# Both Fourier transforms of a transformer trunk over even and odd inputs at 128 frequencies, with the halves combined behind the second one

## What is computed

```
def fourier_mixer(h, w_in, w_out):
    B, S, D = h.shape                                  # 1, 256, 1024
    u = (h @ w_in).reshape(B, S, 4, 256)
    f = jnp.fft.fft2(u.astype(jnp.float32), axes=(1, 3), norm="ortho").real
    return f.astype(h.dtype).reshape(B, S, D) @ w_out
```

## Time and profile before

| | |
|---|---|
| median of 3 runs | 1410.08 us (1409.67 to 1410.91) |
| profiled execution, its own time | 1411.13 us |
| its span, first to last instruction | 1409.3 us |
| mean granted TensorE clock | 0.994 of full |
| PE busy | 1388.9 us (99%), 6511 matmul records |
| DVE busy, ACT busy | 1127.1 us (80%), 926.1 us (66%) |
| HBM | 418.47 MB read, 298 GB/s over the span |

### The profile page before, as it was taken

The page is one execution under the profiler, slowest core; times in us unless marked ns, Lnnn a source line. Parts: engine busy times, 40 slices in busy tenths (PEclk is TensorE's granted clock), DMA queues, the critical chain, the costliest instruction groups (busy, mean ns, idle before and its releaser), DMA issues.

```text
span 1409.3 us, 17766 instructions
## 1 busy us (share of the span) xinstructions
PE 1388.9 (99%) x6511; PEld 1151.1 (82%) x6511; DVE 1127.1 (80%) x811; ACT 926.1 (66%) x760; POOL 20.0 (1%) x29
## 2 busy tenths in 40 slices
PE   9999999999979999999999999999999999999997
PEld 8888888787868888888888888888888888888885
DVE  6455666655668889888988988898898889889887
ACT  6353444444656777777777777777777777777774
POOL 0000000000030000000000000000000000000000
PEclk9999999999989999999999999999999999999999
DMA  9367775563148999999999999999999999999992
GB/s 356 132 179 221 220 202 179 172 198 109 32 140 313 361 375 340 359 377 354 356 362 375 334 362 374 357 357 376 366 329 377 363 354 350 368 375 333 372 375 90
DMA packets 191689, 420.10 MB, mean 298 GB/s; under 512 B 19168, under 2 KB 21344, under 8 KB 191648
## 3 DMA queue, kind: packets, MB, share of 16 engines
q1 hardware_dynamic: 178432, 415.00, 81.9%
q10 hardware_dynamic: 12784, 3.26, 1.7%
q0 software_dynamic: 432, 1.28, 0.3%
HBM read 418.47 MB, written 1.05 MB: 298 GB/s over the span
## 4 chain that ended last, share of the span: by engine, by line
PE 97%; DVE 1%; ACT 1%; DMA 1%; issue 0%; POOL 0%; POOLq 0%; SPq 0%; DVEq 0%; ACTq 0%
PE bank_G L1061 10%; PE bank_G L1063 10%; PE bank_G L1062 10%; PE bank_U L1061 10%; PE bank_U L1063 10%; PE bank_U L1062 10%; PE bank_Y L1061 8%; PE bank_Y L1063 8%; PE bank_Y L1062 8%; PE bank_T L1418 2%; PE bank_G L1310 1%; PE bank_T L1061 1%; PE bank_T L1063 1%; PE bank_T L1062 1%; PE bank_T L1321 1%; PE bank_G L1379 1%
## 5 line engine op out<-in xcount | busy, mean ns | idle before, releaser
L674 DVE TENSOR_TENSOR w_lo<-raw,w_hi 128x2048 fp32r<-128x2048 f32 x390 | 888.0, 2290 | 197.7 <-ACT w_hi L400 197.6
L400 ACT ACTIVATE w_hi<-raw 128x2048 fp32r<-128x2048 f32 x390 | 748.2, 1919 | 284.3 <-PE bank_U L1063 102.1
L1061 PE MATMUL bank_Y<-w_hi,hidT_hi 128*128 128x512 f32 x492 | 192.3, 391 | 0.0
L1063 PE MATMUL bank_Y<-w_hi,hidT_lo 128*128 128x512 f32 x492 | 191.6, 389 | 0.0
L1062 PE MATMUL bank_Y<-w_lo,hidT_hi 128*128 128x512 f32 x492 | 191.4, 389 | 0.0
L1061 PE MATMUL bank_U<-w_hi,xg_hi 128*128 128x512 f32 x448 | 179.1, 400 | 0.0
L1061 PE MATMUL bank_G<-w_hi,xg_hi 128*128 128x512 f32 x448 | 175.7, 392 | 0.7 <-DVE w_lo L674 0.5
L1063 PE MATMUL bank_U<-w_hi,xg_lo 128*128 128x512 f32 x448 | 175.0, 391 | 0.0
L1063 PE MATMUL bank_G<-w_hi,xg_lo 128*128 128x512 f32 x448 | 174.8, 390 | 0.0
L1062 PE MATMUL bank_G<-w_lo,xg_hi 128*128 128x512 f32 x448 | 174.7, 390 | 0.0
L1062 PE MATMUL bank_U<-w_lo,xg_hi 128*128 128x512 f32 x448 | 174.6, 390 | 0.0
(11 more groups left out here) (264 smaller groups left out, 1471.1 us busy)
## 6 DMA issues: line engine op xcount, KB each, us to landing
raw<-in_expert_w_gate SPq DMA_DIRECT2D x112, 1024.0 KB, 7.0
raw<-in_expert_w_up SPq DMA_DIRECT2D x112, 1024.0 KB, 7.0
raw<-in_expert_w_down SPq DMA_DIRECT2D x112, 1024.0 KB, 6.8
raw<-in_nat_w_qkv SPq DMA_DIRECT2D x12, 1024.0 KB, 5.1
raw<-in_ffn_w_gate SPq DMA_DIRECT2D x11, 1024.0 KB, 7.9
raw<-in_ffn_w_up SPq DMA_DIRECT2D x11, 1024.0 KB, 6.0
raw<-in_ffn_w_down SPq DMA_DIRECT2D x11, 1024.0 KB, 5.2
raw<-in_fourier_w_in SPq DMA_DIRECT2D x4, 1024.0 KB, 11.5
```

The lines of the kernel that those rows point to most:

```text
L400: nc.scalar.activation(w_hi[w][:], raw[s][:], ACT.Copy).then_inc(hi_made, 1)
L674: nc.vector.tensor_tensor(w_lo[w][:], raw[s][:], w_hi[w][:].bitcast(f32), ALU.subtract).then_inc(lo_made, 1)
L1061: nc.tensor.matmul(out_, xh, wh, start=start, stop=False)
L1063: return nc.tensor.matmul(out_, xl, wh, start=False, stop=stop)
```

## The change

A 256-point sum over inputs splits into a sum over even inputs and one over odd inputs; the second half of the output frequencies is the first sum minus the second. Both transforms are now made so, at 128 frequencies:

- x is loaded a first time into `x_turns` with token 2p+b in partition p, so that block b is the tokens of one parity, and a second time into `h`, behind the table, for the addition at the end. The table has 3 x 128 columns, its rows sorted even first.
- `u_hi` and `u_lo` are written with the even channels of a group before the odd ones: the reads of the banks step by two elements (`by_parity`).
- `token_dft` gives 128 cosines and 128 sines for each token parity b, side by side in the bank and not accumulated: 6 matmuls of 256 columns.
- `channel_dft(g)` gives, for the even channels (r = 0) and the odd ones (r = 1), 128 frequencies of the group: 12 matmuls of 256 columns for a whole group, into one bank Y[g % 2]. The moving operand is taken in two runs of 128 columns.
- ScalarE copies the odd half to SBUF (`odd`). VectorE's `fold` adds and subtracts it (`by_channel`, two operations of 256 elements), then adds and subtracts the token parities (`by_token`, two more). ScalarE and VectorE make `act_hi` and `act_lo` of a group at once, 512 elements, one turn of the loop later.
- The projection's first piece waits for two groups, its second piece for all four.

Cut to its core:

```diff
+    fo |= layout([("x_turns", [P, NB, D], f32), ("dft_raw", [P, NB, 3 * P], f32)],
+                 arena_start + sum(width_of(shape) for _, shape, _ in fourier_l[:4]))
+    def by_parity(bk):
+        return bk[:].rearrange("p (j r) -> p r j", r=2)
+    def u_part(t, c, b):
+        return t[:, b, BANK * c:BANK * (c + 1)].rearrange("p (r j) -> p r j", r=2)
...
         for c in range(2):
-            sp.dma_start(h[:, :, cs], x[0, :, cs].rearrange("(b p) d -> p b d", p=P)).then_inc(s_x[c], 16)
+            sp.dma_start(fo["x_turns"][:, :, cs], x[0, :, cs].rearrange("(p b) d -> p b d", b=NB)).then_inc(s_x[c], 16)
...
             if j == 3:
                 sp.dma_start(fo["dft_raw"][:], dft_c.rearrange("(b p) n -> p b n", p=P)).then_inc(s_dft, 16)
+                sp.dma_start(h[:], x[0].rearrange("(b p) d -> p b d", p=P)).then_inc(s_h, 16)
...
-                nc.scalar.activation(fo["u_hi"][:, b, BANK * c:BANK * (c + 1)], (G, U)[c][b][:], ACT.Copy,
+                nc.scalar.activation(u_part(fo["u_hi"], c, b), by_parity((G, U)[c][b]), ACT.Copy,
...
-        for g in range(KD // 2 + 1):
-            for m in (2 * g, 2 * g + 1) if g < KD // 2 else ():
+        for g in range(GROUPS + 2):
+            for m in (2 * g, 2 * g + 1) if g < GROUPS else ():
                 act.wait_ge(pt_psum, m + 1)
                 if m >= PT:
-                    act.wait_ge(ft_psum, m // 2 * 2 - PT + 2)
+                    act.wait_ge(ft_psum, (m - PT) // 2 + 1)
                 nc.scalar.activation(fo["pt_hi"][:, m % PT], T[m % 2][:], ACT.Copy).then_inc(pt_hi_done, 1)
-            for m in (2 * g - 2, 2 * g - 1) if g else ():
-                act.wait_ge(ft_psum, m + 1)
-                nc.scalar.activation(act_hi[:, m], Y[m % 2][:, :S], ACT.Copy).then_inc(ft_hi_done, 1)
+            if g >= 2:
+                act.wait_ge(ft_tokens, 2 * (g - 1))
+                nc.scalar.activation(act_hi[:, 2 * g - 4:2 * g - 2],
+                                     fo["by_token"][:, g % 2].rearrange("p k b t -> p k (b t)"), ACT.Copy).then_inc(ft_hi_done, 1)
+            if 1 <= g < GROUPS + 1:
+                act.wait_ge(ft_psum, g)
+                if g >= 3:
+                    act.wait_ge(ft_channels, 2 * (g - 2))
+                nc.scalar.activation(fo["odd"][:, (g - 1) % 2], Y[(g - 1) % 2][:, S:], ACT.Copy).then_inc(ft_odd, 1)
...
+            if pieces is at["w_out"]:
+                dve.wait_ge(s_h, 16)
...
+        def fold(g):
+            even, odd = Y[g % 2][:, :S], fo["odd"][:, g % 2]
+            channels, tokens = fo["by_channel"][:, g % 2], fo["by_token"][:, g % 2]
+            dve.wait_ge(ft_odd, g + 1)
+            for n, op in enumerate((ALU.add, ALU.subtract)):
+                nc.vector.tensor_tensor(channels[:, n].rearrange("p b t -> p (b t)"), even, odd, op).then_inc(ft_channels, 1)
+            dve.wait_ge(ft_channels, 2 * (g + 1))
+            for n, op in enumerate((ALU.add, ALU.subtract)):
+                nc.vector.tensor_tensor(tokens[:, :, n], channels[:, :, 0], channels[:, :, 1], op).then_inc(ft_tokens, 1)
...
             for b in range(NB):
-                last = three(T[m % 2][:], fo["u_hi"][:, b, P * m:P * (m + 1)], fo["u_lo"][:, b, P * m:P * (m + 1)],
-                             fo["dft_hi"][:, b, 0:2 * S], fo["dft_lo"][:, b, 0:2 * S], b == 0, b == NB - 1)
+                last = three(T[m % 2][:, S * b:S * (b + 1)], fo["u_hi"][:, b, o:o + P], fo["u_lo"][:, b, o:o + P],
+                             fo["dft_hi"][:, b, 0:S], fo["dft_lo"][:, b, 0:S], True, True)
...
+        def channel_dft(g):
+            pe.wait_ge(pt_lo_done, 2 * g + 2)
+            if g >= 2:
+                pe.wait_ge(ft_channels, 2 * (g - 1))
+            for r in range(2):
+                for part in range(2):
+                    o = (0, S)[part]
+                    moving = [fo[name][:, (2 * g + r) % PT].rearrange("p (b f t) -> p b f t", b=NB, f=2)[:, :, part]
+                              for name in ("pt_hi", "pt_lo")]
+                    last = three(Y[g % 2][:, S * r:S * (r + 1)].rearrange("p (b t) -> p b t", b=NB),
+                                 fo["dft_hi"][:, r, o:o + P], fo["dft_lo"][:, r, o:o + P], *moving, part == 0, part == 1)
             last.then_inc(ft_psum, 1)
...
-        pe.wait_ge(ft_lo_done, KD)
-        project(at["w_out"][0], G, BANK, fo_psum)
+        def folded(n, b):
+            if b == 0:
+                pe.wait_ge(ft_lo_done, GROUPS // 2 * (n + 1))
+        project(at["w_out"][0], G, BANK, fo_psum, folded)
```

More of the change, by code:

```diff
@@ L177, in trunk @@
     bias_l = [("bias", [P, HEADS * SHIFTS, GRID], f32)]
-    fourier_l = [("dft_hi", [P, NB, 3 * S], f32r), ("dft_lo", [P, NB, 3 * S], f32r),
+    fourier_l = [("dft_hi", [P, NB, 3 * P], f32r), ("dft_lo", [P, NB, 3 * P], f32r),
                  ("u_hi", [P, NB, D], f32r), ("u_lo", [P, NB, D], f32r),
-                 ("pt_lo", [P, PT, 2 * S], f32r), ("pt_hi", [P, PT, 2 * S], f32r)]
+                 ("pt_lo", [P, PT, 2 * S], f32r), ("pt_hi", [P, PT, 2 * S], f32r),
+                 ("odd", [P, 2, S], f32), ("by_channel", [P, 2, 2, NB, P], f32), ("by_token", [P, 2, 2, NB, P], f32)]
     attn_l = bias_l + [("qT", [P, KD, S], f32), ("kT", [P, KD, S], f32),
@@ L231, in trunk @@
     s_x = [sem(f"s_x{c}") for c in range(2)]
+    s_h = sem("s_h")
     h_half, sq_done, rstd_chain, rstd_done, hn_done = (sem(n) for n in (
@@ L743, in _ @@
                 dve.wait_ge(u_hi_done, NB * c + b + 1)
-                cs = slice(BANK * c, BANK * (c + 1))
-                rest_scaled(fo["u_lo"][:, b, cs], (G, U)[c][b][:], rstd[:, 0, b:b + 1], fo["u_hi"][:, b, cs]).then_inc(u_lo_done, 1)
+                rest_scaled(u_part(fo["u_lo"], c, b), by_parity((G, U)[c][b]), rstd[:, 0, b:b + 1], u_part(fo["u_hi"], c, b)).then_inc(u_lo_done, 1)
             if c == 0:
@@ L748, in _ @@
                 rest(fo["dft_lo"][:], fo["dft_raw"][:], fo["dft_hi"][:]).then_inc(dft_lo_done, 1)
-        for g in range(KD // 2 + 1):
-            for m in (2 * g, 2 * g + 1) if g < KD // 2 else ():
+        def fold(g):
[7 more added lines that the diff above has]
+                nc.vector.tensor_tensor(tokens[:, :, n], channels[:, :, 0], channels[:, :, 1], op).then_inc(ft_tokens, 1)
+        for g in range(GROUPS + 2):
+            for m in (2 * g, 2 * g + 1) if g < GROUPS else ():
                 dve.wait_ge(pt_hi_done, m + 1)
                 rest(fo["pt_lo"][:, m % PT], T[m % 2][:], fo["pt_hi"][:, m % PT]).then_inc(pt_lo_done, 1)
-            for m in (2 * g - 2, 2 * g - 1) if g else ():
-                dve.wait_ge(ft_hi_done, m + 1)
-                rest(act_lo[:, m], Y[m % 2][:, :S], act_hi[:, m]).then_inc(ft_lo_done, 1)
+            if g >= 2:
+                dve.wait_ge(ft_hi_done, g - 1)
+                rest(act_lo[:, 2 * g - 4:2 * g - 2], fo["by_token"][:, g % 2].rearrange("p k b t -> p k (b t)"),
+                     act_hi[:, 2 * g - 4:2 * g - 2]).then_inc(ft_lo_done, 1)
+            if 1 <= g < GROUPS + 1:
+                fold(g - 1)
         n = at["w_out"][0][-1]
@@ L1098, in transpose_stream @@
                         kk = 2 * q + k
-                        last = nc.tensor.transpose(STREAM[i][q][:, o:o + P], h[:, b, P * kk:P * (kk + 1)], ident[:])
+                        of = h if i else fo["x_turns"]
+                        last = nc.tensor.transpose(STREAM[i][q][:, o:o + P], of[:, b, P * kk:P * (kk + 1)], ident[:])
                 last.then_inc(tr_done, 1)
@@ L1159, in channel_dft @@
             last.then_inc(ft_psum, 1)
-        for g in range(KD // 2 + 1):
-            for m in (2 * g, 2 * g + 1) if g < KD // 2 else ():
+        for g in range(GROUPS + 1):
+            for m in (2 * g, 2 * g + 1) if g < GROUPS else ():
                 token_dft(m)
-            for m in (2 * g - 2, 2 * g - 1) if g else ():
-                channel_dft(m)
-        pe.wait_ge(ft_lo_done, KD)
-        project(at["w_out"][0], G, BANK, fo_psum)
+            if g:
+                channel_dft(g - 1)
@@ L1512, in shape_constants @@
 def shape_constants():
-    turn = 2 * np.pi * (np.outer(np.arange(S), np.arange(S)) % S) / S
+    turns = np.concatenate([np.arange(0, S, 2), np.arange(1, S, 2)])
+    turn = 2 * np.pi * (np.outer(turns, np.arange(P)) % S) / S
     cos, sin = np.cos(turn) / np.sqrt(S), np.sin(turn) / np.sqrt(S)
```

11 lines of the change are left out of this document (7 added, 4 removed).

## The result

The changed kernel takes 1400.51 us (median of 4 runs, 1399.99 to 1401.18), the one before 1409.93 us (median of 4, 1409.67 to 1410.91): a ratio of 0.9932, 95% interval 0.9919 to 0.9944. It is faster by 9.4 us, where 9.6 had been forecast (1400.4). The profiled execution of the changed kernel took 1400.22 us, with a span of 1398.0.

The account below looks back on a forecast made before the run. TensorE, 97% of the chain, bounds the kernel; after the change VectorE bounds the transform stage. w_out starting at 47.59 instead of 57.23 takes 9.64 us off 1410.08, giving 1400.4 us; range 1398.8 to 1404.5.

Parts of the forecast that it names:

- TensorE's part: Both transforms: 96 matmuls of 256 columns at 0.12 us, 11.5 us; 10.9 us of matmuls go.
- The split operand: Rival, channel products: two runs of 128 columns lose the fast format, 0.53 us a matmul, 1418.5 us, slower; chance 0.04.
- VectorE's part: Transform loop: VectorE needs 3.6 us a turn against TensorE's 2.9 us and becomes the bound of the stage.
- The loads: Ahead of w_out: 0.66 MB more to load, 1.7 us at 389 GB/s, without moving the start or delaying the stage.
- The start does not move: Program start: x and pieces 0 to 3 are ahead of the added loads, so no delay there.
- Hidden, by some 2 us: Load of piece 4: lands about 22.9 instead of 21.2 us; ScalarE takes it up only at 25.08.
- second cover: Piece 5 on ScalarE: taken up at 28.17 us, having waited for TensorE, not for data.
- The walk: Transform stage followed wait by wait: last channel product ends and w_out starts at 47.59 instead of 57.23, 9.64 us earlier.
- What must hold behind it: w_out: last act_lo ready 0.5 us before the second piece, w_lo of piece 6 with 2.5 us of cover; cost nothing.
- The step of two in PSUM: u_hi and u_lo reading PSUM by two: taken as free; at half rate 0.96 us, 1401.4 us in all.
- The clock: Rival, transform stage: waits of 1.0 and 1.4 us make the granted clock fall, 1411.2 us, no change; chance 0.05.
- lost behind the mixer: Rival, after the transforms: piece 6 or a load is late, up to 3 us lost, 1403.5 us; chance 0.04.

Follow-up runs that it names:

- e13: Changed kernel with x_turns read in the pattern of the kernel before (tokens then in the wrong order for the table); 1399.86 us, single execution.
- e16: Changed kernel with act_lo of group 0 behind the last two pt_lo, x_turns in one whole-row load, h loaded behind piece 7; 1400.46 us, ratio 0.9931.
- e6: Changed kernel with two more VectorE operations of by_token's shape in each fold, into a spare buffer; 1401.64 us, single execution.
- e17: Changed kernel run again unedited, on the same chip as e16; 1400.58 us, ratio 0.9930 to the kernel before.

## Why the prediction was right, point by point

**TensorE's part** held: 0.12 us for each of the 96 matmuls of 256 columns, whether the moving operand is one run or two. The split operand, the rival on the slower side, did not come: 283 to 292 ns of duration and 0.12 us apart, as before.

**VectorE's part** was right in kind and a little dear. The single durations met to 0.01 us (0.417 for 0.425, 0.422 for 0.416, 0.687 for 0.684). The turn was taken at 3.6 us and measured 3.27 (41.35 to 44.62, first `pt_lo` to first `pt_lo`): six of its seven operations start 0.08 us before the end of the one in front (the first `by_token` waits for `by_channel` and starts 0.04 behind it), where the sum took off 0.12 in all. From the end of the last `u_lo` to the end of the last `pt_lo` the walk had 10.96 us, and the profile has 10.26 (35.64 to 45.90), with VectorE's two waits at 1.55 us, as foreseen (1.5). The difference is the 0.7 us by which the stage was shorter than forecast (13.53 for 14.24). One sign did not come: VectorE was to have no idle time until 51. Behind the last `pt_lo` it waits twice for `act_hi`, 0.70 us each, ahead of the `act_lo` of groups 2 and 3; this is off the way to the start of `w_out`.

**The loads** were the step that failed, twice. "The start does not move": it moved, by 0.60 us in the two profiles compared here, through the way in which `x_turns` is read (e13, e16), a cost that the prediction did not have: it reasoned from the order of the loads, and 0.37 us of it is SyncE issuing them. "Hidden, by some 2 us": piece 4 came at 25.9 and not 22.9, and ScalarE waited for it. One more issue was taken at nothing, as SyncE waits on the queue anyway; but SyncE came to the first issue of `w_out` at 10.86 us instead of 9.12, 1.23 of it for issuing the load of h. How much of the 3 us that is stays open, as the 22.9 came from a rate and no row showed the landing of piece 4 before. Its second cover did the work: `w_hi` of piece 5 waits for TensorE until 28.8 whatever piece 4 does, so the last `u_lo` did not move against TensorE.

**The walk** ended at 47.59 and the kernel at 47.49, which is better than its parts were: +0.61 at the start and -0.71 in the stage nearly cancel. That the two are 0.1 us apart is luck.

**What must hold behind it** held. `act_lo` of the last group ended at 52.2, 0.7 us ahead of the second piece (0.5 foreseen), and `w_lo` of piece 6 began at 53.3, in VectorE's timeline:

```profile
51.51 0.69 DVE L716 TENSOR_TENSOR act_lo<-by_token,act_hi 128x512 fp32r<-128x512 f32 x1 [0.70 <-ACT act_hi L493]
53.31 4.49 DVE L695 TENSOR_TENSOR w_lo<-raw,w_hi 128x2048 fp32r<-128x2048 f32 x2 [1.11 <-ACT w_hi L414]
```

e6 shows how thin the first cover is: with 0.68 us more a group on VectorE the second piece waits. No run used up the second, that of piece 6.

**The step of two in PSUM** was taken at nothing, and cost nothing: the last `u_hi` and `u_lo` took 690 and 749 ns. The 1.0 us of half rate was not there. The Trainium skill, Advanced Engine Details and Errata, section PSUM Cachelines, says of matmuls that an access which is not contiguous slows them, and gives no price. Here ScalarE and VectorE were the readers and lost nothing; whether it holds for matmuls no run here shows.

**The clock** stayed at 1.00 in the stage. The two idles of 0.73 and 0.72 us between groups of matmuls did not make it fall. The Trainium skill, TensorE: Matmul & The Clock Gate, section on psum-queue depth-cycling, speaks of idles that come frequently, which two in 13.5 us are not, so this stage neither bears it out nor contradicts it.

**The rest of the program** moved as a block: the attention's first product came 9.91 us earlier (320.89 for 330.80), the first matmul of the routing that waits 4.1 us 9.92 us (403.61 for 413.53). No gain was lost behind the mixer. The two profiled executions differ by 10.9 us, 1.3 more than the forecast; that came later, in the routing and behind it, and is not the change's (last section).

## What to carry to other kernels

When a matmul stage is halved, add up the turn of every other engine at once, from start to start: the bound passes to the next engine before the matmuls are gone, and the gain stops there (the halves' 4.53 and 5.49 us became 9.25). Before adding up two edits, take out what both contain: here 1.1 us. A result that is wanted in two parts should be waited for in two parts, above all when its tail is a chain of small operations: here that alone was worth 4.85 us of the stage and 7.6 of the median time, the clock that a 4.7 us wait lost included. And a changed load order is not free because it moves the same bytes: look at the issues and the GB/s of the first microseconds.

## What was not expected of the hardware

**The read pattern of x.** From 4 to 6 us the loads ran at 315 GB/s when a partition takes the half rows of two neighbouring rows (296 to 332 in the nine profiles that read so), at 375 when it takes two that are 128 rows apart (368 to 375 in three), and at 369 when it takes two neighbouring rows whole, in one load (e16). `w_in` is behind x in the same queue, so these are rates of the queue and not of x alone. SyncE's time to issue x differs too: 1.32, 0.96 and 0.39 us. Why is open; the runs tell the patterns apart, not the cause.

**The clock's return differs between executions of one kernel.** In the routing TensorE waits 4.1 us and the granted clock falls to half. In the profiled execution of the changed kernel it was back before 410 us; in e17, the same kernel, only after 412, so that the expert stage's first matmuls at 411.6 still ran at half speed. Table by stretch of the first,

```profile
408.00:410.00 2.00, 1.46 (x6) 0.50 (x5) 2.00 (x2) 0.84 (x2) 0.00 (x0) 0.78 0.00 0
410.00:412.00 2.00, 1.43 (x8) 1.10 (x9) 1.31 (x3) 0.95 (x2) 0.00 (x0) 1.00 0.51 57
412.00:414.00 2.00, 2.00 (x10) 1.68 (x9) 2.00 (x2) 0.00 (x0) 0.00 (x0) 1.00 1.02 418
```

and of e17:

```profile
408.00:410.00 2.00, 1.74 (x6) 0.74 (x5) 2.00 (x2) 0.60 (x1) 0.00 (x0) 0.50 0.00 0
410.00:412.00 2.00, 1.61 (x6) 1.12 (x6) 0.99 (x2) 1.09 (x2) 0.00 (x0) 0.50 0.42 92
412.00:414.00 2.00, 2.00 (x6) 1.56 (x6) 1.86 (x2) 0.11 (x1) 0.00 (x0) 0.56 1.01 412
```

The two executions took 1400.22 and 1401.76 us, with `w_out` at 47.49 and 47.45. The kernel before shows the late return in its profile (0.56 from 422 to 424 us). At the expert stage's first wait for `w_lo` they stand at 423.11 and 424.56, so nearly all of the 1.54 us between them arose in the routing. The kernel before stands there at 434.49, 11.4 us behind the changed one, where it had been 9.9 behind at the start of the routing; 0.5 us of that is made up later. So up to 1.5 us of a difference between two single executions of this kernel is the clock in the routing, as much as the better of the edits above gains.
